# Gate weight sums of a Strassen-like product: copies issued by SyncE, and another order around the attention heads

## The reference

```python
h = rmsnorm(x, attn_norm_g)
z = h @ w_in
gates = sigmoid(h @ w_gate + b_gate)              # 1024 x 3072
y_a = gmlp_mixer(z[..., :512], ...)
y_b = pool_mixer(z[..., 512:768], ...)
y_c = diff_attn_mixer(q, k, v, ...)               # 4 heads, two softmaxes each, blended
merged = g_a * (y_a @ proj_a) + g_b * (y_b @ proj_b) + g_c * (y_c @ proj_c)
x = x + merged @ w_out
```

## Time and profile before

| what | us |
|---|---|
| median of 3 runs | 1463.52 (1463.35 to 1465.45) |
| the profiled execution | 1465.08 |
| its span | 1462.6 |
| TensorE busy | 1416.9 (97%) |
| VectorE busy | 1113.6 (76%) |
| ScalarE busy | 796.9 (54%) |
| GpSimd busy | 104.0 (7%) |

### The profile page before, as it was taken

The page is one execution under the profiler, slowest core; times in us unless marked ns, Lnnn a source line. Parts: engine busy times, 40 slices in busy tenths (PEclk is TensorE's granted clock), DMA queues, the critical chain, the costliest instruction groups (busy, mean ns, idle before and its releaser), DMA issues.

```text
span 1462.6 us, 23129 instructions
## 1 busy us (share of the span) xinstructions
PE 1416.9 (97%) x8993; PEld 1259.7 (86%) x8993; DVE 1113.6 (76%) x1613; ACT 796.9 (54%) x1136; POOL 104.0 (7%) x129
## 2 busy tenths in 40 slices
PE   9999696989999999999999999999999999999998
PEld 7878695978889999999988787778888889999896
DVE  4868565567699879969876776877565697978888
ACT  6436464632656556546563555535443865748474
POOL 0111111000000100010000000000000000010100
PEclk9999898999999999999999999999999999999999
DMA  8879887542447766586243233233211768585761
GB/s 302 276 213 264 213 255 195 168 168 87 138 122 218 190 183 173 153 227 154 80 176 116 87 119 111 73 101 101 73 58 58 212 164 231 142 240 149 223 152 72
DMA packets 63974, 235.48 MB, mean 161 GB/s; under 512 B 7256, under 2 KB 7768, under 8 KB 63236
## 3 DMA queue, kind: packets, MB, share of 16 engines
q1 hardware_dynamic: 46752, 167.01, 33.2%
q0 software_dynamic: 12864, 56.11, 19.3%
q10 hardware_dynamic: 4260, 11.00, 2.2%
HBM read 231.96 MB, written 31.23 MB: 180 GB/s over the span
## 4 chain that ended last, share of the span: by engine, by line
PE 82%; DMA 9%; issue 5%; DVE 2%; POOL 1%; ACT 1%; SPq 0%; POOLq 0%; DVEq 0%; ACTq 0%
PE ps L2356 26%; PE ps L2357 25%; PE ps L2358 25%; DMA gate_sums<-gates_dram 6%; DMA gate_sums<-gate_sums 2%; PE ps L4025 1%; POOL gate_sums L2238 1%; PE ps L2520 1%; PE ps L2535 1%; PE ps L3925 1%; POOL gate_sums L2235 0%; PE ps L2408 0%; DMA tables<-tables_dram 0%; DVE y L3718 0%; PE ps L4045 0%
## 5 line engine op out<-in xcount | busy, mean ns | idle before, releaser
L966 ACT ACTIVATE wh<-stage 128x1024 fp32r<-128x1024 f32 x147 | 154.8, 1056 | 236.6 <-PE ps L2358 202.4
L2357 PE MATMUL ps<-hl,wh 128*128 128x256 f32 (+1 forms) x832 | 276.5, 332 | 0.0
L2356 PE MATMUL ps<-hh,wh 128*128 128x512 f32 (+1 forms) x760 | 260.0, 342 | 0.1
L2358 PE MATMUL ps<-hh,wl 128*128 128x512 f32 (+1 forms) x760 | 256.3, 337 | 0.0
L1484 DVE TENSOR_TENSOR wl<-stage,wh 128x1024 fp32r<-128x1024 f32 x146 | 177.7, 1221 | 72.5 <-ACT wh L966 72.4
L2357 PEld LDWEIGHTS ps<-hl,wh 128*128 128x128 f32 x832 | 158.2, 190 | 13.5
L2356 PEld LDWEIGHTS ps<-hh,wh 128*128 128x128 f32 x760 | 144.3, 190 | 17.9 <-issue 2.9
L2358 PEld LDWEIGHTS ps<-hh,wl 128*128 128x128 f32 x760 | 144.3, 190 | 15.5
L3013 ACT ACTIVATE wh<-raw 128x1024 fp32r<-128x1024 f32 x75 | 78.7, 1054 | 50.8 <-PE ps L2358 44.7
L3605 DVE TENSOR_TENSOR wl<-raw,wh 128x1024 fp32r<-128x1024 f32 x75 | 90.9, 1219 | 20.2 <-ACT wh L3013 19.8
L1919 DVE TENSOR_TENSOR wl<-raw,wh 128x1024 fp32r<-128x1024 f32 (+1 forms) x75 | 88.7, 1186 | 22.4 <-ACT wh L1263 21.8
(11 more groups left out here) (519 smaller groups left out, 3812.5 us busy)
## 6 DMA issues: line engine op xcount, KB each, us to landing
stage<-stream_dram SPq DMA_DIRECT2D x110, 512.0 KB, 3.3
raw<-up_dram SPq DMA_DIRECT2D x64, 512.0 KB, 7.1
raw<-down_dram SPq DMA_DIRECT2D x52, 512.0 KB, 6.0
gate_sums<-gates_dram POOLq DMA_DIRECT2D x36, 512.0 KB, 7.7
stage<-gate_sums SPq DMA_DIRECT2D x24, 512.0 KB, 4.1
stage<-gates_dram SPq DMA_DIRECT2D x18, 512.0 KB, 7.0
raw_sum<-up_dram SPq DMA_DIRECT2D x16, 512.0 KB, 3.4
raw_sum<-up_dram POOLq DMA_DIRECT2D x16, 512.0 KB, 8.4
```

Of the source, the lines that this page charges most:

```text
L966: A(parts_of(b, p)[0], b.stage[:, p.stage, :], ACT.Copy).then_inc(s.hi_ready, 1)
L2356: MM(out, wh, xh, start=start, stop=False, skip_group_check=True)
L2357: MM(out, wh, xl, start=False, stop=False, skip_group_check=True)
L2358: return MM(out, wl, xh, start=False, stop=stop, skip_group_check=True)
```

## The change

- The bases of all four sums of a group (24 copies of 512 KB in all, out of `gates` only) are issued by SyncE, four for a group, behind the loads of rows 9, 10, 12, 13, 15 and 16. Before groups 2 and 4 SyncE waits until the copies of the pair before have landed. They count on `gate_bases`.
- GpSimd only adds. P6's base is weight block 2, to which Q5's sum is added; R4's base is block 3, to which P6's sum is added. A pair has three rounds: four additions, two, two. It starts when its bases have landed and the pair before is done.
- TensorE runs the first two score blocks of a head in Q5 at piece 4 and the other two in P6 at piece 5; the values go in P1 at piece 2 in place of 4. The waits for the head's operands move there as well (`head_start`).
- ScalarE: `vh` ahead of `gate_seed`; the exponentials of blocks 0 and 1 ahead of `gate_copy(Q5)`, those of blocks 2 and 3 ahead of `gate_copy(P6)`. In group 5, `ych` ahead of `hi` of the fifth row.
- VectorE: both first score pairs ahead of the `lo` of the group's first two rows, blocks 2 and 3 ahead of the third; `blend` ahead of both `gate_sub`. In group 5, `head_rest` ahead of the `lo` of the sixth row.

```diff
+SUM_LEVEL = {Q5: 4, P7: 4, P6: 6, R4: 8}
+SUM_BASE = {Q5: 0, P6: 2, R4: 3, P7: 1}
...
+    def sum_bases(g):
+        if g % 2 == 0 and g:
+            sp.wait_ge(s.gate_bases.sem, s.gate_bases.at(64 * g))
+        for product, r in SUM_BASE.items():
+            sp.dma_start(dram["gate_sums"][g, GATE_SUM[product]],
+                         dram["gates"][g, r]).then_inc(s.gate_bases.sem, 16)
+
+    bases = {9: 0, 10: 1, 12: 2, 13: 3, 15: 4, 16: 5}
     for row in range(2 * RING, P_GATE):
         load_row(row, row - RING)
+        if row in bases:
+            sum_bases(bases[row])
...
-        gate_seed(i)
         if i:
             act.wait_ge(s.pv_done, i)
         AR(b.vh[:], b.v[:, :, P * i:P * i + P], ACT.Copy).then_inc(s.v_hi, 1)
+        gate_seed(i)
         hi(Panel(first))
+        exps(i, 0)
+        exps(i, 1)
         gate_copy(i, Q5)
         hi(Panel(first + 1))
         if i == 0:
             gate_hi("X12")
-        exps(i, 0)
-        exps(i, 1)
+        exps(i, 2)
+        exps(i, 3)
         gate_copy(i, P6)
         hi(Panel(first + 2))
         if i == 0:
             gate_hi("X22")
-        exps(i, 2)
-        exps(i, 3)
...
-        lo(Panel(first))
         dve.wait_ge(s.v_hi, i + 1)
...
         score_pair(i, 0, 0, (b.bias, b.bias))
+        score_pair(i, 1, 0, (b.bias, b.bias))
+        lo(Panel(first))
         lo(Panel(first + 1))
-        score_pair(i, 1, 0, (b.bias, b.bias))
         if i == 0:
             gate_rest_of("X12")
-        lo(Panel(first + 2))
         for qb in (2, 3):
             score_pair(i, qb, 0, (b.bias, b.bias))
+        lo(Panel(first + 2))
         if i == 0:
             gate_rest_of("X22")
+        blend(i)
         gate_sub(i, Q3)
-        blend(i)
         gate_sub(i, P7)
...
     for pair in range(GATE_GROUPS // 2):
         groups = (2 * pair, 2 * pair + 1)
+        pool.wait_ge(s.gate_bases.sem, s.gate_bases.at(128 * pair + 128))
         if pair:
-            summed(16 * pair)
+            summed(8 * pair)
         for g in groups:
-            copied(g, 0, dram["gates"][g, 0])
-            copied(g, 3, dram["gates"][g, 1])
-        summed(16 * pair + 4)
+            added(g, Q5, dram["gates"][g, 1])
+            added(g, P7, dram["gates"][g, 2])
+        summed(8 * pair + 4)
         for g in groups:
-            added(g, 0, 1)
-            added(g, 3, 2)
-        summed(16 * pair + 8)
+            added(g, P6, dram["gate_sums"][g, GATE_SUM[Q5]])
+        summed(8 * pair + 6)
         for g in groups:
-            copied(g, 1, dram["gate_sums"][g, 0])
...
+            added(g, R4, dram["gate_sums"][g, GATE_SUM[P6]])
...
-            between = {P6: {0: [sc(g, 0), sc(g, 1)]}, Q3: {3: [sc(g, 2), sc(g, 3)]},
+            between = {Q5: {4: [head_start(g), sc(g, 0), sc(g, 1)]}, P6: {5: [sc(g, 2), sc(g, 3)]},
                        R4: {1: [tn(g, 0), tn(g, 1)], 4: [tn(g, 2)], 6: [tn(g, 3)]}}
             if g:
-                between[P1] = {4: [pv(g - 1)]}
+                between[P1] = {2: [pv(g - 1)]}
```

More of the change, by code:

```diff
@@ L402, in semaphores @@
     s.gate_sums = Counted(s.gate_summed, 0)
+    s.gate_bases = Counted(s.lines_set, 1)
     s.gate_copied = Counted(s.line_copied, 1)
@@ L690 @@
 GATE_BLOCK = {P1: 0, Q3: 2, P2: 3}
-SUM_LEVEL = {Q5: 8, P7: 8, P6: 12, R4: 16}
+SUM_LEVEL = {Q5: 4, P7: 4, P6: 6, R4: 8}
+SUM_BASE = {Q5: 0, P6: 2, R4: 3, P7: 1}
 def gate_panel(g, product):
@@ L823, in sync_program @@
         if product in GATE_SUM:
-            sp.wait_ge(s.gate_sums.sem, s.gate_sums.at(256 * (g // 2) + 16 * SUM_LEVEL[product]))
+            sp.wait_ge(s.gate_sums.sem, s.gate_sums.at(128 * (g // 2) + 16 * SUM_LEVEL[product]))
             source = dram["gate_sums"][g, GATE_SUM[product]]
@@ L1199, in scalar_program @@
         hi(Panel(first + 3))
+        if g == 5:
+            for h in range(4):
+                act.wait_ge(s.o_normed, h + 1)
+                A(b.ych[:, h, :], b.o[:, h, :], ACT.Copy, scale=b.subln).then_inc(s.yc_hi, 1)
         if g == 4:
@@ L1206, in scalar_program @@
         gate_differences(g)
[L1207 to L1210, removed]
         hi(Panel(first + 6))
@@ L1844, in vector_program @@
                             ALU.add).then_inc(s.omean_ready, 1)
-        gate_lo(5)
         if g == 5:
@@ L1848, in vector_program @@
                 head_rest(h)
+        gate_lo(5)
         gate_lo(6)
@@ L2232, in summed, with added @@
         pool.wait_ge(s.gate_sums.sem, s.gate_sums.at(16 * count))
[L2234 to L2238, removed]
+    def added(g, product, source):
+        G.dma_start(dram["gate_sums"][g, GATE_SUM[product]], source, accum_op=ALU.add,
                     max_dma_last_dim=4 * D).then_inc(s.gate_sums.sem, 16)
@@ L2594, in tn, with head_start, step @@
         return lambda: turn(i, kb, s.turned_ready)
+    def head_start(i):
+        def step():
+            pe.wait_ge(s.qk_ready, i + 1)
+            pe.wait_ge(s.yab_written, 4)
+            if i:
+                pe.wait_ge(s.o_evac, i)
+        return step
     def pv(i):
@@ L2606, in tensor_program @@
         if g < 4:
-            between = {P6: {0: [sc(g, 0), sc(g, 1)]}, Q3: {3: [sc(g, 2), sc(g, 3)]},
+            between = {Q5: {4: [head_start(g), sc(g, 0), sc(g, 1)]}, P6: {5: [sc(g, 2), sc(g, 3)]},
                        R4: {1: [tn(g, 0), tn(g, 1)], 4: [tn(g, 2)], 6: [tn(g, 3)]}}
             if g:
-                between[P1] = {4: [pv(g - 1)]}
+                between[P1] = {2: [pv(g - 1)]}
         elif g == 4:
-            between = {P1: {4: [pv(3)]}, P7: {0: [square_sums]}, R4: {0: [turn_sums]}}
+            between = {P1: {2: [pv(3)]}, P7: {0: [square_sums]}, R4: {0: [turn_sums]}}
         else:
@@ L2615, in tensor_program @@
         for product in ORDER1:
[L2616 to L2620, removed]
             gate_item(g, product, between.get(product, {}))
```

## The result

| what | before | after |
|---|---|---|
| median of 7 runs, us | 1465.06 (1463.35 to 1466.79) | 1457.08 (1453.09 to 1460.26) |
| ratio of the runs | 1 | 0.9944 (95%: 0.9926 to 0.9961) |
| the profiled execution, us | 1465.08 | 1460.26 |
| its span, us | 1462.6 | 1458.2 |
| TensorE busy, us | 1416.9 | 1414.6 |

The change makes the kernel 8 us faster. The forecast was 24.7 us, to 1439 us, and the measured time lies above the range of 1430 to 1447.

What follows compares the result with a forecast made beforehand. TensorE was taken as the bound nearly everywhere, with savings only between 100 and 310 us. The terms 24.5 - 1.5 - 4.5 + 6.2 = 24.7 us gave a median of 1439 us, range 1430 to 1447 (1425 to 1454 with rivals 1, 2, 4).

Steps and rivals of the forecast that it cites:

- Part 1, the gain: Weight-sum copies moved from GpSimd to SyncE: both long turn waits in groups 1 and 3 go, 24.5 us together.
- The pair's pace: GpSimd's weight sums: with only additions left, a pair takes 44 to 50 us where it took 71.
- The turn's own chain: Turns of the probabilities, TensorE: what limits next once the long waits for the sums are gone, as group 2 shows.
- Part 1, the price of the copies: SyncE's queue, rows 9 to 17: 22 us of DMA added, 18 free or less; 1.5 us of waiting, between 0 and 15.
- SyncE's wait: SyncE waits for the first eight copies before issuing the next, with rows 13 to 18 behind; no separate price.
- Rival 2: SyncE's queue: copies hold up the weights, 5 to 15 us late near rows 16 to 18; about 1451 us, chance 0.17.
- Rival 3: SyncE's queue: a copy costs what an addition does, 3.5 us, so the kernel is slower, 1477 us; chance 0.06.
- Rival 4: GpSimd's addition rounds stretch, P6 levels still 4 to 6 us late in groups 1 and 3; 1450 us, chance 0.05.
- Part 2: New head orders: P7 waits for P6's copy behind exponentials; costs 4.5 us, between a gain of 12 and loss of 8.
- the 1 us that was to come back: Clock behind the waits ahead of R4: two shorter waits may leave TensorE at full clock, 1 us credited to part 2.
- Part 3: Group 5: earlier `ych` cuts the wait ahead of the projections to 0.2 us; gain 3.6 + 2.6 = 6.2 us with clock.
- The sign of rival 2: TensorE waiting for `wl` between 80 and 115 us would show that the copies hold up the weights.

Runs made afterwards that it cites:

- the last kernel: Against the kernel with spread copies and old head orders: both subtractions ahead of the blend on VectorE, turns later on TensorE; 1425.6 us, 0.9744 of the kernel before.

## Why the prediction was wrong

*Part 1, the gain.* Right. Forecast 24.5 us; groups 1 and 3 gained 12.3 and 12.7. The pair's pace was right too: 44 to 50 us were forecast, and pair 1 took from 136.09 to 181.16 = 45.1 us:

```profile
84.69 0.84 POOL L2247 DMA_DIRECT2D gate_sums<-gates_dram  x1 [28.75 <-issue]
...
136.09 0.82 POOL L2247 DMA_DIRECT2D gate_sums<-gates_dram  x1 [9.07 <-DMA gate_sums<-gate_sums]
...
181.16 1.66 POOL L2247 DMA_DIRECT2D gate_sums<-gates_dram  x2 [6.86 <-DMA gate_sums<-gate_sums]
```

Its start was not: 106 to 115 was forecast. The first pair's fourth addition was issued at 84.69 only, 28.75 us behind the other three, and all its rounds ran beside the copies. The groups were late by 21 us as well, and so this cost nothing more. "The turn's own chain" was what came next, as forecast (3.6 us in three waits, 2.1 at the most). The reserve was smaller than forecast, though: with the copies spread, pair 1 took from 119.80 to 173.28 = 53.5 us, and its P6 level came at 158.3, where the forecast had 147.

*Part 1, the price of the copies.* **This is the step that failed**: 1.5 us of waiting, with bounds of 0 and 15. It was 19.4 us to P1 of group 0 (131.52 against 112.1) and 21.1 to its Q5, with the half clock behind the waits. The price of one copy was nearly right. Over 34 to 53 us q1's share of 91.3% is 17.3 us of 16 engines, for 5.90 MB, which are eight copies and some three loads: 1.54 us for each 512 KB. A load costs between 1.33 (its bytes at 387 GB/s and 0.98 busy) and 1.8 us (28.0% of 6.5 us for the load between 84.4 and 90.9 before), so a copy costs 1.4 to 1.6 (an estimate), where 1.4 was taken. Even the sum was there: 22 us added, 18 free or less. What failed is the step from "the engines are full" to "1.5 us". A mean over 75 us was set against a load's reserve, but a load waits for what stands in front of it at its issue. Rows 16 and 17 had the thinnest reserve, as the forecast said, and eight copies ahead of a load are 8 x 1.54 = 12 us, if nothing else uses the engines. The rule should have been: bytes in front of this load in its queue, over the share that the queue gets. Between 60 and 83 us the queues' shares were (packets, MB, share)

```profile
q1 hardware_dynamic: 529, 4.23, 50.2%
q0 software_dynamic: 398, 1.44, 35.4%
```

so SyncE's queue (q1) had half, and GpSimd's (q0) 35.4%; ScalarE's, with the bias lines, had another 12.7%. The Trainium skill ("DMA: Bandwidth & Descriptors", section "Queues, rings and completion order") has an engine take packets from the queues that have work in turn; the forecast named it and left it out for want of a row. These rows agree with it in the share: half of a full engine was what was left beside the additions and the bias lines. The rows with the copies in ScalarE's queue agree more closely: 152, 157 and 153 packets of three queues in one stretch, for 56.1, 29.4 and 16.2% of the engines. By the measured share of 50.2% the eight copies issued from 52.90 on and the load among them, 9 x 1.54 = 13.9 us of the engines, take 27.6 us; they were in when SyncE went on, 30.3 us later.

*SyncE's wait.* The forecast named it and what stood behind it, and gave it no price. It was 5 of the 19.4 us.

*Rival 2* had the mechanism and a chance of 0.17, at 1451 us; its terms were 5 to 15 us. It is the case that happened, some 6 us dearer. Rival 3's price (3.5 us a copy) is excluded by the 1.54. Rival 4 did not happen: `hi` of P6 in groups 1 and 3 had its loads in time.

*Part 2.* Sign and mechanism right, size wrong. Forecast 4.5 us, bound 8. In group 0 it was 3.5 (forecast 4.1), in group 1 0.1, and in groups 2 and 3 5.1, nearly all of it in group 2, where 1.4 were taken for three groups. The term that was mis-sized is the bias tile's landing: the sum set it "as late as it can" at 7.6 us, from a stretch of the kernel before, and among the moved copies and additions it was 8.8. A longer wait also cost clock. In the kernel with spread copies the stretches behind P7's waits of 1.05 us (group 1) and 3.26 us (group 2) show (us; busy time of TensorE's matmuls, its weight loads, VectorE, ScalarE and GpSimd; granted clock, DMA share, GB/s)

```profile
162.00:165.00 3.00, 3.00 (x28) 3.00 (x27) 2.44 (x6) 1.56 (x3) 0.00 (x0) 1.00 0.78 141
193.50:196.50 3.00, 3.00 (x15) 3.00 (x16) 2.34 (x6) 1.54 (x2) 0.00 (x0) 0.50 0.93 244
```

From R4 to the next Q5, groups 1 and 3 took 9.7 us each at a granted clock of 1.00, where the old orders took 10.4 at 0.84: 0.6 us came back twice. In group 2, from P7 to R4, the new orders took 8.3 us with no wait in them, and the old ones 5.9 beside their wait of 2.1: 2.4 us went. In sum, the 1 us that was to come back didn't. In the changed kernel's group 0 the P7 wait was 2.2 us and not 5, since the late P1 had given the bias time to land.

*Part 3.* Right: 6.2 forecast, 3.6 + 2.5 in the trace, 5.2 alone between medians.

*The signs that it named.* No wait ahead of the projections and none of `hi` for `gate_sums` in groups 1 and 3: so it was. The longest wait ahead of P7 was to be 5 us in group 0; it was 3.65 us in group 2. The sign of rival 2, TensorE waiting for `wl` between 80 and 115 us, came as waits for the eviction `qk`, which stands behind such a `lo` on VectorE.

With the sizes of the traces in place (25.0 and 6.1 for the gains of parts 1 and 3, 21.1 for 1.5, and 1.3 + 3.9 for groups 0 and 2) the sum is 25.0 + 6.1 - 21.1 - 5.2 = 4.8 us, as between the profiled executions.

What stays open: between the medians the change gained 8.0 us, 3.2 more than between the profiled runs. Its runs lie 7 us apart, those of before 3.4; where that comes from was not looked into. The share that SyncE's queue gets was read from two stretches only, and the split of the 19.4 us into wait, order and bytes rests on one trace for each kernel.

## What to carry to other kernels

Price a DMA that is moved into a queue by the loads that stand behind it there: for each, the bytes in front of it over the queue's share of the engines, against its own reserve. A mean of the DMA engines' free share over a long stretch says only whether the total fits. A burst of plain copies is cheap one by one and holds a deadline load back by all of them; one copy between two loads didn't here. Another issuing engine's queue takes away only what stands in front of the load, not the division of the engines: beside the copies in ScalarE's queue, SyncE's had 16.2% of them.

An edit on one chain can't be priced in a kernel where another chain ends later. The new heads' orders, which seemed to cost nothing, cost 8 to 10 us once the sums were in time; take the later chain away first, and then compare. And where an engine does long work of its own ahead of a short one that TensorE waits for, as the blend ahead of the subtraction, put the short one first and move the consumers of the long one.

## What the runs showed of the hardware

- A DRAM-to-DRAM copy of 512 KB costs 1.4 to 1.6 us of all 16 DMA engines from SyncE's queue (an estimate, from 17.3 us for 5.90 MB) and 1.3 from GpSimd's; the accumulating one 3.5.
- Three queues at work at once moved nearly equal numbers of packets (152, 157, 153) and very unequal bytes (2.46, 0.58, 0.54 MB), in the kernel with ScalarE's queue, 91.5 to 103 us.
- GpSimd's issue of a DMA itself can stand: 28.75 us ahead of the fourth accumulating DMA in the row at 84.69 above (releaser "issue"), with three of them under way beside the second eight plain copies. In the kernel with ScalarE's queue it was 13.57. In both the fourth was issued 0.3 us behind the landing of the third (84.44 and 64.71), and so it was in the kernel before (75.79 and 75.54).
- Waits of TensorE of 2.1 us went either way. With old orders and spread copies R4 waits 2.13 us in groups 1, 2 and 3, and the three stretches behind have a granted clock of 0.57, 1.00 and 0.50 (columns as above):

```profile
165.50:168.50 3.00, 3.00 (x18) 3.00 (x17) 3.00 (x5) 2.02 (x4) 0.82 (x1) 0.57 0.39 59
195.00:198.00 3.00, 2.65 (x22) 2.45 (x22) 3.00 (x4) 2.03 (x4) 0.23 (x1) 1.00 0.72 93
224.00:227.00 3.00, 3.00 (x17) 3.00 (x16) 2.87 (x4) 1.99 (x4) 0.00 (x0) 0.50 0.40 94
```

  With waits of at most 1.4 us, in the last kernel, the clock of the stretch 136 to 300 us is 1.00.
